# Recurrent level products that stream the queries' columns only

## The chip, the cores and the metric

The kernel runs on one core of one Trainium2 chip. The metric is the device time of one launch in microseconds (us), as the median of several runs. The engines are named as the profile names them: PE is TensorE's matmul, PEld its weight load (the load of the stationary operand into the array), DVE is VectorE, ACT is ScalarE, POOL is GpSimd, SP is SyncE, which issues the transfers.

## The reference, cut to what matters

The program computes two transformer-like blocks, one after the other, on 1024 tokens of width 1024. The change touches one part of the second block, a gated linear recurrence with 4 heads of width 128, run forwards and backwards:

```python
causal = jnp.tril(jnp.ones((HG_CHUNK, HG_CHUNK), bool))[:, :, None]
...
    b = jnp.cumsum(gc, axis=2)
    inter = jnp.einsum('bhtk,bhkv->bhtv', qc * jnp.exp(b), s)
    diff = b[:, :, :, None, :] - b[:, :, None, :, :]
    decay = jnp.where(causal, jnp.exp(jnp.minimum(diff, 0.0)), 0.0)
    scores = jnp.einsum('bhtk,bhtsk,bhsk->bhts', qc, decay, kc)
    intra = jnp.einsum('bhts,bhsv->bhtv', scores, vc)
```

A score between query t and key s holds a decay that differs for each of the 128 features, so the scores aren't one plain matrix product.

## The kernel before

The kernel is a sequence of stages. `stage_hgrn` computes the recurrence in 8 units, `units[n] = (h, d)`: head h (0 to 3), direction d (0 forwards, 1 backwards); even n are forwards. The 1024 tokens lie along the free axis, the 128 features across the partitions, in 8 chunks of 128 tokens.

The scores of a chunk are built from 7 levels, `LEVELS = [64, 32, 16, 8, 4, 2, 1]`, and a diagonal. At a level with runs of m tokens the chunk is cut into blocks of 2m; one half of each block holds keys, the other queries. For d = 0 the keys are the left half and the queries the right, for d = 1 the other way round. Both are decayed to the middle of their block, so that one float32 matmul of the buffer with itself holds all scores between the two halves. Level 0 (m = 64) has one block in a chunk: 64 adjacent key tokens and 64 adjacent query tokens. At level 6 (m = 1) keys and queries alternate.

For each unit and level:

- DVE subtracts (`subtract`, L3198/L3199 or L3202/L3203) and ACT takes the exponential (L3034), in one of three buffers `x`.
- DVE multiplies the keys' half (L3211) and the queries' half (L3212) in (`weigh`). The second of these raises `x_ready`.
- PE waits for `x_ready` in `level`, then issues 8 matmuls, one for each chunk, 128 stationary columns against 128 moving columns (L2914). Each float32 matmul is two weight loads and two passes in the records, so a level is 16 of each.
- DVE copies the scores that the mask of this level names into `att` (`select`, L3229). It reads the queries' columns of PSUM only. The diagonal (L3237) is taken first, from a product of its own (L2935).

PE's jobs rotate over three pairs of PSUM banks (`slot`: job number modulo 3), so a job starts only when the job three before it has been read (`wait_free`). PE's order in unit n is written out by hand: transposes of the decayed keys (L2932), the diagonal's product (L2935), levels 0 and 1, in units 2, 4 and 6 a sum of squares (L2922), the chunks' states (L2945), the projections Z0 and Z1 of unit n+1 (L200), levels 2 and 3, the product with the states (L2956), the projection V0 when unit n+1 begins a head, level 4, the other projections of unit n+1 (GATE for a backwards unit, V1 and QUERY for a forwards one), levels 5 and 6, and then, after `selected`, the product of the scores with the values (L2967). `selected` is raised by DVE when `select` of level 6 is done.

After Z1, ACT and DVE prepare unit n+1: ACT takes out Z1 (L2980), three activations (L3015 to L3017), DVE L3147 to L3149, and, after ACT's L3026 to L3028 (`forget_parts`, which comes behind the take-out of V0 in ACT's order), DVE's `forget` (L3158 to L3166) and `key_distance` (L3176), with `select` of levels 5 and 6 behind that. In some other stages PE runs narrower products: L2668 has 128 stationary columns and one moving column, L475 one or two stationary columns and 64 moving ones in four column groups in turn, L1336 64 stationary columns in two column groups in turn.

Of the kernel before, what the change touches and what calls it, by code (L numbers as in the profile page):

```python
# [26 lines left out]
P = 128  # L27
T = 1024
# [37 lines left out]
LEVELS = [64, 32, 16, 8, 4, 2, 1]  # L66
# [751 lines left out]
class SsmParams:  # L818
# [26 lines left out]
    def product(self, out, a, b, t):  # L845

        link, tt = self.link, self.dve.tensor_tensor
        link(tt(t[0], a[0], b[0], ALU.mult))
        link(tt(t[1], a[1], b[1], ALU.mult))
        link(tt(t[2], a[0], b[1], ALU.mult))  # L850
        link(tt(t[3], a[1], b[0], ALU.mult))
        link(tt(out[0], t[0], t[1], ALU.subtract))
        link(tt(out[1], t[2], t[3], ALU.add))
# [1910 lines left out]
def stage_hgrn(k):  # L2764
# [13 lines left out]
    def take(*shape):  # L2778
        v = k.ar(at[0], *shape)
        at[0] += int(np.prod(shape))  # L2780
        return v
# [4 lines left out]
    keys, b = take(2, TT), take(2, TT)  # L2786
# [11 lines left out]
    units = [(h, d) for h in range(HG_HEADS) for d in range(2)]  # L2798
# [27 lines left out]
    def slot(job):  # L2826
        i = jobs.index(job)
        return i % 3, i // 3

    def banks(job):  # L2830
        s, _ = slot(job)
        return k.ps[:, 2 * s:2 * s + 2, :].rearrange("p b n -> p (b n)")
# [4 lines left out]
    def wait_free(pe, job):  # L2837
        s, use = slot(job)
        if use >= 1:
            pe.wait_ge(read[s], use)  # L2840
# [13 lines left out]
    def buffer(n, l):  # L2854
        return (NL * n + l) % 3
# [7 lines left out]
    out = k.second_out = OutProjection(k, "w_out_2", None, 16 * T, B_FREE, first_raw=k.ar(B_FREE + 2 * T, 2, KD, P),  # L2863
                                       first_tile=HG_HEADS)
# [4 lines left out]
    with nc.Block() as block:  # L2869
# [13 lines left out]
        def _(pe):  # L2883
# [21 lines left out]
            def chunk_job(job, chunks, fn):  # L2905
                wait_free(pe, job)
                for i, c in enumerate(chunks):
                    last = fn(banks(job)[:, i * P:(i + 1) * P], c)
                last.then_inc(made[slot(job)[0]], 1)

            def level(n, l):
                pe.wait_ge(x_ready, NL * n + l + 1)
                v = x[:, buffer(n, l), :]
                chunk_job((n, "level", l), range(T // P), lambda out, c: pe.matmul(  # L2914
                    out, v[:, c * P:(c + 1) * P], v[:, c * P:(c + 1) * P], start=True, stop=True))

            def sum_of_squares(n, h):
                pe.wait_ge(sq_done, h)
# [9 lines left out]
            for n, (h, d) in enumerate(units):  # L2928
                halves = (range(8), range(8, NCH))
                pe.wait_ge(kh_ready, n + 1)  # L2930
                for i in range(2):
# [4 lines left out]
                    out, keys[:, n % 2, CTX + c * P:CTX + (c + 1) * P], q[:, h % 2, c * P:(c + 1) * P],  # L2936
                    start=True, stop=True))
                level(n, 0)
                level(n, 1)
                if d == 0 and h:  # L2940
                    sum_of_squares(n, h)
# [5 lines left out]
                front(n + 1, Z0)  # L2947
                front(n + 1, Z1)
                level(n, 2)
                level(n, 3)  # L2950
                pe.wait_ge(states_ready, n + 1)
# [3 lines left out]
                for c in range(T // P):  # L2955
                    last = pe.matmul(o_ps[:, c * P:(c + 1) * P], states[:, c, :], qh[:, c * P:(c + 1) * P],  # L2956
                                     start=d == 0 and c % 4 == 0, stop=False, skip_group_check=True)
# [8 lines left out]
                for c in range(T // P):  # L2966
                    last = pe.matmul(o_ps[:, c * P:(c + 1) * P], vals[:, h % 2, CCH + c, :], att[:, c * P:(c + 1) * P],  # L2967
                                     start=False, stop=d == 1, skip_group_check=True)
# [728 lines left out]
```

## Time and profile before

| what | value |
|---|---|
| median of the 3 runs | 2686.35 us |
| lowest and highest run | 2682.31 and 2688.17 us |
| span of the profiled execution | 2683.6 us |
| PE busy, share of the span | 2515.2 us, 94% |
| DVE, ACT busy | 1618.7 us, 961.3 us |
| `stage_hgrn`'s units | about 1398 to 1830 us |
| level products, L2914 | 448 matmuls as 896 passes |

For the profiled execution only the span from first to last instruction is given; it lies 2.75 us under the median of the runs and 1.3 us over the fastest of them. Busy times are unions of the recorded intervals. The mean of one instruction holds its latency and overlaps with its neighbours, so the pace of a stream of n equal instructions is read as (busy time of the group minus one duration) / (n - 1).

### The profile page before, as it was taken

To read this page: it belongs to the slowest core of one execution; us is meant where nothing else is said; L and a number is where in the kernel's file an instruction comes from. 1 tells how busy PE (TensorE), PEld (TensorE's weight loads), DVE (VectorE), ACT (ScalarE), POOL (GpSimd) and SP (SyncE) were. 2 spreads that over 40 slices of the span, in tenths; PEclk is the share of its full clock that TensorE was granted. 3 is DMA by queue.
4 is the path that set the end of the run, shared out by engine and by line. 5 is a ranking of instruction groups with operands and counts; after the bars stand their busy time and mean duration, and the time that the engine had idled before them with its cause. 6 is when DMAs were issued, how large, how long until landed. Compare 5 with 4: busy or idle time off the path is not lost. (4 is left out here: it accounts for less than half of the span.)

```text
span 2683.6 us, 39352 instructions
## 1 busy us (share of the span) xinstructions
PE 2515.2 (94%) x16713; PEld 1353.8 (50%) x16713; DVE 1618.7 (60%) x2104; ACT 961.3 (36%) x1116; POOL 26.9 (1%) x60
## 2 busy tenths in 40 slices
PE   7988788999999999999989999988979999999997
PEld 3456564444444444443566776764434444444443
DVE  6687647554444443654447778786766776674253
ACT  5116317432323231423254656563442222222131
POOL 0000000020000000000000000000000000000000
PEclk9999999999999999999999999999989999999999
DMA  9035474111211124432010000002001111123332
GB/s 324 23 99 184 157 228 147 32 32 51 59 47 47 47 80 111 115 94 87 20 32 16 25 24 25 25 16 63 27 15 49 51 47 47 53 62 102 108 102 91
DMA packets 301591, 198.99 MB, mean 74 GB/s; under 512 B 11248, under 2 KB 296078, under 8 KB 301071
## 3 DMA queue, kind: packets, MB, share of 16 engines
q1 hardware_dynamic: 300582, 196.70, 24.8%
q8 instruction: 105, 1.72, 0.3%
q10 hardware_dynamic: 873, 0.32, 0.0%
q14 instruction: 31, 0.25, 0.0%
HBM read 187.02 MB, written 9.45 MB: 73 GB/s over the span
## 5 line engine op out<-in xcount | busy, mean ns | idle before, releaser
L200 PE MATMUL ps<-hT,arena 128*128 128x512 bf16 (+1 forms) x6384 | 1370.9, 377 | 26.4 <-DVE arena L2086 9.9
L200 PEld LDWEIGHTS ps<-hT,arena 128*128 128x128 bf16 x6384 | 624.2, 98 | 770.6 <-issue 32.4
L1907 PE MATMUL ps<-arena 128*128 128x512 bf16 x2112 | 458.7, 379 | 2.7 <-DVE arena L1889 2.5
L1907 PEld LDWEIGHTS ps<-arena 128*128 128x128 bf16 x2112 | 206.3, 98 | 251.8 <-DVE arena L1889 4.9
L2159 DVE SCALAR_TENSOR_TENSOR arena<-ps,vec,arena 128x945 f32<-128x945 f32 (+2 forms) x176 | 215.1, 1222 | 75.0 <-ACT arena L2145 55.6
L2126 DVE SCALAR_TENSOR_TENSOR arena<-ps,vec,arena 128x1023 f32<-128x1023 f32 (+1 forms) x88 | 106.8, 1275 | 179.6 <-ACT arena L2116 179.6
L1889 DVE TENSOR_TENSOR arena<-hT,arena 128x2816 bf16<-128x2816 f32 (+2 forms) x44 | 93.7, 2157 | 164.4 <-ACT arena L1883 164.2
L1883 ACT ACTIVATE arena<-hT 128x2816 bf16<-128x2816 f32 (+2 forms) x44 | 77.8, 1798 | 237.2 <-DMA hT<-w_down_dram 109.5
L2914 PE MATMUL ps<-arena 128*128 128x128 f32 x896 | 109.4, 279 | 12.2 <-DVE arena L3212 11.4
L2073 DVE TENSOR_TENSOR arena<-hT,arena 128x2048 bf16<-128x2048 f32 x44 | 100.9, 2293 | 28.2 <-ACT arena L2040 27.9
L2116 ACT ACTIVATE arena<-ps,vec 128x1024 f32<-128x1024 f32 x44 | 50.6, 1200 | 175.3 <-PE ps L200 175.3
L2914 PEld LDWEIGHTS ps<-arena 128*128 128x128 f32 x896 | 105.3, 194 | 15.5 <-DVE arena L3212 12.9
L2168 ACT ACTIVATE arena<-arena 128x1024 f32<-128x1024 f32 x22 | 23.2, 1056 | 227.2 <-DVEq L2163 227.2
L2086 DVE TENSOR_TENSOR arena<-arena 128x1024 f32 (+1 forms) x44 | 53.9, 1225 | 59.9 <-ACT arena L2052 59.9
L3229 DVE COPY_PREDICATED arena<-masks,ps 128x512 f32<-128x512 uint32 x56 | 49.4, 883 | 62.2 <-PE ps L2914 61.8
L2040 ACT ACTIVATE arena<-hT 128x2048 bf16<-128x2048 f32 x44 | 83.3, 1894 | 8.2 <-DMA hT<-w_up_dram 8.2
L200 PE MATMUL ps<-arena,hT 128*128 128x128 bf16 (+1 forms) x1152 | 78.5, 231 | 6.4 <-PEq L160 6.4
L200 PEld LDWEIGHTS ps<-arena,hT 128*128 128x128 bf16 x1152 | 74.3, 99 | 10.4 <-issue 6.9
L3034 ACT ACTIVATE arena<-arena 128x1024 f32<-128x1024 f32 x56 | 58.3, 1052 | 56.7 <-DVE arena L3203 41.8
L604 ACT ACTIVATE arena<-xT 128x512 f32<-128x512 f32 x64 | 39.8, 630 | 107.8 <-DVE xT L567 54.9
L2980 ACT ACTIVATE arena<-ps 128x1024 f32<-128x1024 f32 (+1 forms) x48 | 36.1, 753 | 118.0 <-PE ps L200 114.6
L1062 PE MATMUL ps<-arena 128*128 128x512 f32 x160 | 71.7, 602 | 0.5
(431 smaller groups left out, 2522.2 us busy)
## 6 DMA issues: line engine op xcount, KB each, us to landing
xT<-ada_w_dram SPq DMA_DIRECT2D x24, 1024.0 KB, 5.5
hT<-w_up_dram SPq DMA_DIRECT2D x44, 512.0 KB, 5.0
hT<-ffn_up_dram SPq DMA_DIRECT2D x44, 512.0 KB, 5.0
hT<-w_down_dram SPq DMA_DIRECT2D x30, 704.0 KB, 7.0
hT<-ffn_down_dram SPq DMA_DIRECT2D x30, 704.0 KB, 6.9
arena<-w_in_dram SPq DMA_DIRECT2D x35, 512.0 KB, 4.1
xT<-w_mod_dram SPq DMA_DIRECT2D x16, 1024.0 KB, 5.8
arena<-w_mod_dram SPq DMA_DIRECT2D x8, 1024.0 KB, 19.4
```

The lines of the kernel that those rows point to most:

```text
L200: last = pe.matmul(out, lhs(a, kt), rhs(b, kt, i), start=start and kt == 0 and (a, b) == (0, 0), stop=stop and kt == n_k - 1 and (a, b) == ...
L1062: last = pe.matmul(k.ps[:, 2 * p + half, :], exact[n][:, kt, :], h[:, kt, half * HALF:(half + 1) * HALF], start=kt == 0, stop=kt == KD - 1)
L1883: last = act.activation(parts[0], raw, ACT.Copy)
L1889: last = dve.tensor_tensor(parts[1], raw, parts[0], ALU.subtract)
L1907: last = pe.matmul(self.bank(u), self.part(u, a, kt), self.g[:, b, kt, cols], start=kt == 0 and (a, b) == (0, 0), stop=kt == FT - 1 and (a ...
L2040: act.activation(self.w[:, b, :, 0], self.raw, ACT.Copy).then_inc(self.hi[b], 1)
L2073: dve.tensor_tensor(self.w[:, b, :, 1], self.raw, self.w[:, b, :, 0], ALU.subtract).then_inc(self.lo[b], 1)
L2086: dve.tensor_tensor(self.g[:, 1, 2 * i + b, :], c[0], self.g[:, 0, 2 * i + b, :], ALU.subtract).then_inc(self.done[b], 1)
L2126: last = eng.scalar_tensor_tensor(c[s][:, lag:T], p[s][:, 0:T - lag], w[:, tap, s, bass.ds(j, 1)], c[s][:, lag:T], ALU.mult, ALU.add)
L2159: eng.scalar_tensor_tensor(to, src[:, r0 + di:r1 + di, c0 + dj:c1 + dj], w[:, 3 * (di + 1) + dj + 1, bass.ds(j, 1)], to, ALU.mult, ALU.add ...
L2914: chunk_job((n, "level", l), range(T // P), lambda out, c: pe.matmul(out, v[:, c * P:(c + 1) * P], v[:, c * P:(c + 1) * P], start=True, st ...
L3034: act.activation(v, v, ACT.Exp).then_inc(exp_done, 1)
```

## The change

Each level product now streams only the queries' columns of a chunk (64 of the 128, every second run of m), and writes them to the columns of PSUM where they stood before, leaving the keys' columns unwritten. The stationary operand stays all 128 columns, except at level 0, where only the 64 columns of the keys are loaded; their scores go to the 64 PSUM partitions (0 to 63 forwards, 64 to 127 backwards) where they stood before. The number and the order of all instructions and waits stay as they were.

```diff
             def level(n, l):
                 pe.wait_ge(x_ready, NL * n + l + 1)
+                d, m = units[n][1], LEVELS[l]
                 v = x[:, buffer(n, l), :]
-                chunk_job((n, "level", l), range(T // P), lambda out, c: pe.matmul(
-                    out, v[:, c * P:(c + 1) * P], v[:, c * P:(c + 1) * P], start=True, stop=True))
+                rows = slice(d * m, (d + 1) * m) if 2 * m == P else slice(0, P)
+                queries = lambda chunk: chunk.rearrange("p (b h r) -> p b h r", h=2, r=m)[:, :, 1 - d, :]
+
+                def product(out, c):
+                    chunk = v[:, c * P:(c + 1) * P]
+                    return pe.matmul(queries(out[rows, :]), chunk[:, rows], queries(chunk), start=True, stop=True)
+
+                chunk_job((n, "level", l), range(T // P), product)
```

## Rows read from the trace of the kernel before

**Rows 1.** The page's costliest groups: busy us, mean ns of one, then idle before
```profile
L2914 PE MATMUL ps<-arena 128*128 128x128 f32 x896 | 109.4, 279 | 12.2 <-DVE arena L3212 11.4
L2914 PEld LDWEIGHTS ps<-arena 128*128 128x128 f32 x896 | 105.3, 194 | 15.5 <-DVE arena L3212 12.9
```

**Rows 2.** Waits from 1400 to 1860 us: us in total, times, longest
```profile
DVE arena L3229 <- PE ps L2914: 61.8, 17, 7.1
...
PE ps L2967 <- DVEq L3320: 21.9, 8, 3.7
...
PE ps L2914 <- DVE arena L3212: 11.4, 8, 5.1
```

**Rows 3.** Timeline around the end of unit 0 and into unit 1: start, duration (us)
```profile
1439.90 3.73 PE L2914 MATMUL ps<-arena 128*128 128x128 f32 x32
...
1443.15 1.49 DVE L3176 TENSOR_TENSOR arena<-arena 128x1280 f32<-128x1280 f32 x1
...
1444.56 2.68 DVE L3229 COPY_PREDICATED arena<-masks,ps 128x512 f32<-128x512 uint32 x2
...
1447.35 3.78 PE L2967 MATMUL ps<-arena 128*128 128x128 f32 x16 [3.71 <-DVEq L3320]
...
1454.66 1.95 PE L2914 MATMUL ps<-arena 128*128 128x128 f32 x16
...
1456.60 0.68 DVE L3212 TENSOR_TENSOR arena<-arena 128x512 f32<-128x512 f32 x1
...
1457.34 2.05 PE L2914 MATMUL ps<-arena 128*128 128x128 f32 x16 [0.73 <-DVE arena L3212]
...
1460.22 0.72 DVE L3229 COPY_PREDICATED arena<-masks,ps 128x512 f32<-128x512 uint32 x1
...
1461.46 13.14 PE L200 MATMUL ps<-hT,arena 128*128 128x512 bf16 x72
```

**Rows 4.** Timeline of the later part of unit 1 and into unit 2
```profile
1490.72 1.02 ACT L2980 ACTIVATE arena<-ps 128x1024 f32<-128x1024 f32 x1 [6.24 <-PE ps L200]
...
1507.38 1.31 DVE L3229 COPY_PREDICATED arena<-masks,ps 128x512 f32<-128x512 uint32 x1 [0.86 <-PE ps L2914]
...
1511.12 2.05 PE L2967 MATMUL ps<-arena 128*128 128x128 f32 x16 [1.98 <-DVEq L3320]
...
1516.02 2.02 PE L2914 MATMUL ps<-arena 128*128 128x128 f32 x16
...
1516.78 1.22 DVE L3237 TENSOR_TENSOR arena<-ps,ident 128x1024 f32<-128x1024 f32 x1
...
1519.25 2.05 PE L2914 MATMUL ps<-arena 128*128 128x128 f32 x16 [1.21 <-DVE arena L3212]
```

**Rows 5.** Timeline at 1322 us, a product with one moving column
```profile
1322.17 0.85 PEld L2668 LDWEIGHTS ps<-ones,arena 1*128 1x128 f32 x7 [0.24 <-issue]
```

**Rows 6.** Timeline at 192 to 194 us, products with few stationary columns
```profile
192.31 0.42 PEld L1336 LDWEIGHTS ps<-arena 128*64 128x64 f32 x8 [0.33 <-issue]
...
193.33 1.07 PE L475 MATMUL ps<-xT,cact 128*1 128x64 f32 x64
```

**Rows 7.** Lines L1336 and L475: instructions, min/median/max ns, first and last start
```profile
L1336 PEld LDWEIGHTS ps<-arena x240: 132/137/230, 192.3 to 276.5; 128*64 128x64 f32 x120
```
```profile
L475 PEld LDWEIGHTS ps<-xT,cact x2560: 79/85/129, 189.6 to 407.8; 128*2 128x2 f32 x118, 128*1 128x1 f32 x79
L475 PE MATMUL ps<-xT,cact x2560: 216/219/314, 189.6 to 407.9; 128*2 128x64 f32 x118, 128*1 128x64 f32 x79
```

**Rows 8.** Busy us of PE, PEld, DVE, ACT, POOL; PEclk, DMA share, GB/s
```profile
207.00:209.00 2.00, 0.19 (x11) 0.10 (x2) 1.83 (x4) 2.00 (x9) 0.00 (x0) 1.00 0.37 96
...
211.00:213.00 2.00, 2.00 (x16) 1.35 (x16) 0.19 (x2) 2.00 (x10) 0.00 (x0) 0.50 0.30 100
```
```profile
1447.00:1449.00 2.00, 1.66 (x8) 1.66 (x8) 1.78 (x3) 0.00 (x0) 0.00 (x0) 0.50 0.01 4
...
1508.00:1511.00 3.00, 1.13 (x11) 0.94 (x9) 3.00 (x4) 1.34 (x2) 0.00 (x0) 1.00 0.56 163
```

## The prediction

> **What bounds the kernel now.** I read the page first: PE is busy in 94% of the span, and the level products, L2914, hold 109.4 us of it, with weight loads for 105.3 us at the same time [rows 1]. That is the most that a change of L2914 could touch. Next come the waits in the recurrent stage. PE waits there in two places only: before L2967 for `selected` (21.9 us in all), and before a level product for DVE's L3212 (11.4 us). DVE waits 61.8 us for L2914, but most of that is level 2, which stands behind the long projections in PE's order [rows 2]. So PE and DVE take turns at setting the end, and each level product has to be placed in the timeline.
>
> In units 0, 2, 4 and 6 (read in unit 0) levels 5 and 6 end at 1443.63, while DVE goes straight from L3176 to the two selects (1444.56 to 1447.24) without a wait for them. PE stands 3.71 us and starts L2967 when they are done [rows 3]. Levels 5 and 6 are off the path there. At the start of the next unit level 0 ends at 1456.61, and level 1 starts only at 1457.34, just after L3212 ends at 1457.28: the 0.73 us after level 0 are DVE's. Then PE runs without a gap: level 1, the states, Z0 and Z1 (to 1474.60), levels 2 and 3 [rows 3].
>
> In units 1, 3 and 5 (read in unit 1) more of PE is on the path. Levels 2 and 3 stand before V0, for which ACT waits 6.24 us before it can go on to the next unit's forget gates; and select of level 5 waits 0.86 us for level 5's product. PE's stop before L2967 is 1.98 us [rows 4]. In the next unit level 1 again waits for L3212, 1.21 us [rows 4].
>
> **The change part by part.** *Nothing is added or moved*: the same instructions, waits and transfers, in the same order. What can change is the pace of a pass, and the latency of the last one.
>
> *The pass before.* 32 passes in 3.73 us at 279 ns each: (3730 - 279) / 31 = 111 ns [rows 1, 3].
>
> *Levels 1 to 6 after.* The streamed columns halve, the loaded columns stay 128. What does a float32 pass cost by its two sides? The load: one stationary column takes 85 ns, 64 take 137, 128 take 194 (the 85 being one or two columns) [rows 1, 7]. That is 85 ns of latency and about 0.83 ns a column, so 128 columns keep the load path for some 107 ns. The stream: 64 passes of 64 moving columns in 1.07 us at 219 ns, (1070 - 219) / 63 = 13.5 ns, in four column groups in turn, so 54 ns in one group [rows 6, 7]. Both sides of today's pass are thus about 107 ns, and the change halves only one. The nearest row to what is left is L2668, 128 loaded columns against a single moving column: seven loads in 0.85 us at about 187 ns (between the 137 for 64 columns and the mean of 194), (850 - 187) / 6 = 110.5 ns [rows 5]. A pass with one moving column is as slow as one with 128; with 64 it can't be far from that. I take 110.5 ns, a gain of 0.5 ns, 0.01 us for a level. The bounds: 54 ns, if the load should somehow not hold it (a gain of 16 x 57 = 0.91 us for a level), and something above 111 if the spread-out columns cost more: DVE's select, which reads the same pattern from PSUM, takes 0.72 us at runs of 32, and 1.31 us at runs of 2 [rows 3, 4], a factor of 1.8. Applied to 54 ns that is 97 ns, still under the load. So I take no loss. The last matmul's latency falls from 279 to some 225 ns (219 for 64 columns [rows 7]), so whoever waits for a level is released about 0.05 us earlier.
>
> A rule speaks against this. The Trainium skill, in SBUF — State Buffer, Door 1: The DMA port swizzle, says that PSUM has lines of 8 bytes and that any non-contiguous pattern there significantly slows down matmuls. No run here shows it for a matmul; it gives no figure, and by the load's 107 ns a slower write would have to be over twice slower before it showed. The sum would move by it only if that is so.
>
> *Level 0 after.* 64 columns loaded (137 - 85 = 52 ns [rows 7]) and 64 streamed (54 ns): 55 to 60 ns a pass, so 16 x 54 = 0.86 us less. Going over to another division of the array costs something: the load before L1336 stood 0.33 us with nothing to wait for [rows 6]. Net about 0.5 us in each unit. All of it goes into the wait behind it: level 1 can't start before L3212, which waits for the diagonal's product and exponentials, not for level 0. The wait of 0.73 us becomes about 1.3, that of 1.21 about 1.7 [rows 3, 4]. The cover is DVE's diagonal and weigh work; were it gone, the term would be worth 8 x 0.5 = 4 us.
>
> *The sum.* On the path lie level 1 in seven units, levels 2, 3 and the release by level 5 in units 1, 3 and 5, and some of the last unit: 3 x (0.05 + 0.05 for V0's earlier start and small pace gains) + 7 x 0.02 + 0.1 = about 0.5 us. The profiled execution's span of 2683.6 us would become 2683.1; against the median of the runs that is 2686.35 - 0.5 = 2685.8 us. What a measurement of this kernel can tell from no change is about 0.2%, 5.4 us.
>
> **The rivals.** *The stream sets the pace (faster).* Then each level is 0.91 us shorter, plus 0.05. For it: 64 streamed columns take 54 ns in L475 [rows 6, 7]. Against it: L2668's 110.5 ns [rows 5]. In the units after an even one only level 1 counts, and Z0 can't begin before select of level 1 has read its banks, 1460.94 against 1461.46 now [rows 3]: about 0.4 us. In units 1, 3 and 5 V0 ends 0.4 + 2 x 0.91 = 2.2 us earlier and the 0.86 us wait for level 5 goes too: 3.1 us. Sum 3 x 3.1 + 4 x 0.4 + 1 for the last unit = 12 us: 2674 us. But PE's stop before L2967 in the odd units then grows from 1.98 to nearly 4 us, and after 3.71 us the even ones run L2967 at half clock (below), about 2 us each: 2680 us. The Trainium skill, in TensorE: Matmul & The Clock Gate, Back-to-back issue gap, gives the isolated gap by the moving columns alone, while its section LDWEIGHTS gives a load by its columns, 128 / 1.2 ns; the first would give this rival, the second the forecast, and the trace's loads agree with the second (107 ns).
>
> *The clock falls more often (slower).* The even units show what it costs: after the stop of 3.71 us the granted clock is 0.50, 1.2 GHz [rows 8], and L2967 takes 3.78 us against 2.05 in unit 1 [rows 3, 4]. From its start to that of level 0 it is 7.31 us (1447.35 to 1454.66) against 4.90 (1511.12 to 1516.02), with the same work between. That is 2.4 us for a fall. In the odd units a stop of 1.98 us leaves the clock at 1.00 [rows 4, 8]. But it is close: at 207 to 209 us PE stood 1.8 us, and the clock was 0.50 at 211 to 213 us although PE had been at work since [rows 8]. After the change PE streams only half of the time in the levels on either side of the stops, and the stops after level 0 grow by 0.5 us. The place is the odd units' stop before L2967; the point from which it decides is a fall there in each of the three: 3 x 2.4 = 7 us, less up to 0.7 us each, since DVE comes to L3237 only at 1516.78 in any case [rows 4]: 5 to 7 us, 2691 to 2693 us. Falls after level 0 in all units, where the states and Z0 would run at half clock, would give up to another 7 x 2 = 14 us, 2707. Against it: the same stops as now, and weight loads busy throughout.
>
> *The spread columns cost more than the load hides (slower).* It decides from 111 ns a pass on; at 160 ns, 0.8 us a level, with levels 4 and 5 on the path in three units, it would be 5 us. I count it with the last.
>
> **How the numbers follow.** Load-bound, clock as now: 0.58, around 2685.8, its own range 2680 to 2690 by the runs' own scatter. Stream-bound: 0.17, 2674 to 2680. Clock or columns: 0.25, 2691 to 2707, most of it near 2693. The range 2677 to 2697 takes in the first, the milder part of the faster one and most of the slower one. Faster by over 0.2% (under 2681): 0.18. Slower (over 2691.7): 0.24. Within: 0.58.
>
> **What the profile after would show.** Right: L2914's loads stay near 100 us busy with 1.8 us for a level; level 0 alone near 1.1 us; the wait for L3212 up by some 4 us; the stop before L2967 unchanged at 3.7 and 2.0 us; selects at the same places of a unit. Stream-bound: a level takes 1.1 us, L2914's idle before it doesn't change by that, and units shorten by 0.4 and 3.1 us. Clock: PEclk 0.5 near L2967 in the odd units or behind level 0, with L2967 above 3 us there. The prediction is wrong if a load isn't the floor that L2668 shows, or if half-streamed passes count for less with the clock.

## The result and the profile after

The changed kernel takes 2703.35 us (median of 4 runs, 2698.32 to 2707.68) against 2685.89 us before (4 runs): 1.0066 of before, 95% interval 1.0051 to 1.0082. It is slower by some 17 us, where 2685.8 and at most 2697 had been forecast. The profiled execution has a span of 2696.6 us, 13.0 more than before; it is the fastest of the four, so it shows a little less than the whole loss.

The level products first. They are L2920 now, the other lines of the stage move down by 7 (L2939 are the transposes, L2942 the diagonal's product, L2952 the chunks' states, L2929 the sum of squares, L2963 the product with the states, L2974 the product with the values). These are the page's costliest groups after, in the columns of [rows 1]:

```profile
L2920 PE MATMUL ps<-arena 128*128 128x64 f32 (+1 forms) x896 | 103.3, 273 | 17.6 <-DVE arena L3219 17.0
...
L2920 PEld LDWEIGHTS ps<-arena 128*128 128x128 f32 (+1 forms) x896 | 100.5, 190 | 20.9 <-DVE arena L3219 19.0
```

Half of the columns are gone, and 6 us of 109 with them. The wait for DVE's last multiplication (L3219, which was L3212) grew by 5.6 us, about as much. (The 103.3 us hold some 2 us of level 1 at half clock, in units 3 and 5.) So PE's own work and wait at this line cancel, as forecast, and the 13 us must be elsewhere.

The timeline after, PE alone, at the start of unit 1, to be laid beside [rows 3]:

```profile
1453.87 1.15 PE L2920 MATMUL ps<-arena 128*64 128x64 f32 x16
1456.51 2.00 PE L2920 MATMUL ps<-arena 128*128 128x64 f32 x16 [1.49 <-DVE arena L3219]
1458.34 4.08 PE L2952 MATMUL ps<-arena 128*128 128x128 f32 x20
...
1475.24 3.68 PE L2920 MATMUL ps<-arena 128*128 128x64 f32 x32
```

Level 0 takes 1.15 us instead of 1.95, and the stop behind it 1.49 instead of 0.73. Levels 2 and 3 take 3.68 us instead of 3.74, at 64 columns a pass. Between them stands the loss: L2952, which the change doesn't touch, takes 4.08 us for its 20 passes. Before, the same product (L2945) took 2.40 us, with the clock at 1.00:

```profile
1459.23 2.40 PE L2945 MATMUL ps<-arena 128*128 128x128 f32 x20
```
```profile
1457.00:1460.00 3.00, 2.66 (x23) 2.66 (x24) 3.00 (x6) 0.87 (x1) 0.00 (x0) 1.00 0.02 5
```

What happened to it after is in the table by stretches (columns as in [rows 8], the granted clock is the number behind POOL's):

```profile
1457.00:1459.00 2.00, 2.00 (x18) 2.00 (x18) 2.00 (x5) 0.70 (x1) 0.00 (x0) 0.87 0.03 8
1459.00:1461.00 2.00, 2.00 (x11) 2.00 (x11) 2.00 (x4) 0.36 (x1) 0.00 (x0) 0.50 0.00 0
1461.00:1463.00 2.00, 1.95 (x12) 1.64 (x12) 0.62 (x3) 1.06 (x1) 0.00 (x0) 0.77 0.00 0
```

PE is busy all the time, and the clock drops to 0.50, 1.2 GHz, while it works. In the 2 us at that clock 11 passes go through, against 18 in the 2 us before, at 0.87. Three other places after:

```profile
1511.81 2.62 PE L2974 MATMUL ps<-arena 128*128 128x128 f32 x16 [1.98 <-DVEq L3327]
...
1574.61 3.68 PE L2920 MATMUL ps<-arena 128*128 128x64 f32 x16 [1.87 <-DVE arena L3219]
1578.08 4.03 PE L2952 MATMUL ps<-arena 128*128 128x128 f32 x20
...
1762.22 3.63 PE L2929 MATMUL ps<-arena,ones 128*128 128x512 f32 x4
```

The first is the stop between two units, 1.98 us as before, but the product behind it takes 2.62 us instead of 2.05 [rows 4], and the transposes behind it (L2939) 2.34 us instead of 1.25. The others stand behind level 1. The seven intervals between the starts of the product with the values sum to 394.5 us (1446.58 to 1841.12), against 379.4 before (1447.35 to 1826.75), 15.1 us more. That is more than the whole difference of the spans; the rest of the kernel is 2 us shorter in this execution. Unit 2 has no fall behind level 1. In units 1, 3, 4, 5, 6 and 7 the stretch from the start of level 1 to the start of level 2 is 1.6, 3.2, 1.7, 1.6, 1.7 and 1.6 us longer than before, 11.5 us together. The last unit loses 1.5 us more in L2963. Behind the slow L2974 of units 1, 3 and 5 the stretch up to the next level 1 is 0.96 us longer each, 2.9 us together; the other differences are under 1 us each and nearly cancel.

### The profile page after: what moved, and what is told of

It is laid out like the page before. It is cut to its first block and busy times, and to the rows that moved or that the text cites. A ratio compares the mean times of both kernels' runs of the same rounds, so it can differ in the third digit from the quotient of the medians.

```text
span 2696.6 us, 39175 instructions
## 1 busy us (share of the span) xinstructions
PE 2509.7 (93%) x16536; PEld 1361.3 (50%) x16713; DVE 1619.1 (60%) x2104; ACT 961.7 (36%) x1116; POOL 26.9 (1%) x60
## 5 line engine op out<-in xcount | busy, mean ns | idle before, releaser
L200 PE MATMUL ps<-hT,arena 128*128 128x512 bf16 (+1 forms) x6255 | 1357.1, 376 | 36.4 <-DVE arena L2086 9.9
L2920 PE MATMUL ps<-arena 128*128 128x64 f32 (+1 forms) x896 | 103.3, 273 | 17.6 <-DVE arena L3219 17.0
L2920 PEld LDWEIGHTS ps<-arena 128*128 128x128 f32 (+1 forms) x896 | 100.5, 190 | 20.9 <-DVE arena L3219 19.0
```

What stands on the lines that cost most here:

```text
L200: last = pe.matmul(out, lhs(a, kt), rhs(b, kt, i), start=start and kt == 0 and (a, b) == (0, 0), stop=stop and kt == n_k - 1 and (a, b) == ...
L2920: return pe.matmul(queries(out[rows, :]), chunk[:, rows], queries(chunk), start=True, stop=True)
```

## The experiments

All ratios are to the kernel before on the same chip, with 95% intervals. Each diff is against the changed kernel, unless the text says that it is against the kernel before. A fall is a place where the clock goes to half and the products take longer; each timeline shows one execution. "Theory 1" is that passes that stream half of the time bring the clock down near PE's stops, "Theory 2" that the longer stop after the coarsest level does.

**Levels 1 to 6 changed, level 0 as before.**

```diff
-                rows = slice(d * m, (d + 1) * m) if 2 * m == P else slice(0, P)
-                queries = lambda chunk: chunk.rearrange("p (b h r) -> p b h r", h=2, r=m)[:, :, 1 - d, :]
+                rows = slice(0, P)
+                queries = lambda chunk: chunk if l == 0 else chunk.rearrange("p (b h r) -> p b h r", h=2, r=m)[:, :, 1 - d, :]
```

> Levels 1 to 6 stream the queries' columns only; level 0 is as in the kernel before. Theory 1 (passes that stream half of the time bring the clock down at the stops near them): PE still stops 2.0 us before L2967's product in the odd units between two half-streamed levels, and the clock falls there as in the changed kernel, and behind level 1 in most units: 1.004 to 1.007 of before. Theory 2 (the longer stop after the coarsest level does it): that stop is back at 0.7 to 1.2 us, so 1.000 to 1.002.

Measured: 1.0013 (1.0004 to 1.0022). Six of seven levels are as in the changed kernel and four fifths of the loss are gone. Nothing falls behind level 1 (L2952 takes 2.39 to 2.45 us in all units); the odd units' product with the values takes 2.9 to 3.8 us, and the last unit's L2963 3.68 us:

```profile
1459.35 2.00 PE L2920 MATMUL ps<-arena 128*128 128x64 f32 x16 [0.82 <-DVE arena L3219]
1461.18 2.45 PE L2952 MATMUL ps<-arena 128*128 128x128 f32 x20
...
1513.02 3.40 PE L2974 MATMUL ps<-arena 128*128 128x128 f32 x16 [1.98 <-DVEq L3327]
```

Taken alone this speaks for Theory 2.

**Level 0 changed alone.**

```diff
-                queries = lambda chunk: chunk.rearrange("p (b h r) -> p b h r", h=2, r=m)[:, :, 1 - d, :]
+                queries = lambda chunk: chunk if l else chunk.rearrange("p (b h r) -> p b h r", h=2, r=m)[:, :, 1 - d, :]
```

> Only level 0 is changed (64 columns loaded, 64 streamed); levels 1 to 6 stream all 128 columns. Theory 1: all passes next to the stops stream fully but those of level 0, so the odd units' product with the values stays near 2.05 us and the time near 1.000 to 1.002 of before. Theory 2: the stop after level 0 is 1.4 us long as in the changed kernel, the states' product behind it takes over 3.5 us in half of the units, 1.003 to 1.006.

Measured: 0.9993 (0.9984 to 1.0002), no difference that can be told. The odd units' product with the values is at 2.05 us, as Theory 1 had it. Theory 2's loss doesn't come in the median. The profiled execution is one of the longer ones (2689.54 us against a median of 2684.64). In it units 1, 2 and 3 have falls behind level 0 all the same, after stops of 1.87, 2.10 and 1.88 us; units 4 and 6 stand as long, 2.11 and 2.12 us, and have none. Unit 2:

```profile
1518.48 1.12 PE L2920 MATMUL ps<-arena 128*64 128x64 f32 x16
1521.70 2.52 PE L2920 MATMUL ps<-arena 128*128 128x128 f32 x16 [2.10 <-DVE arena L3219]
1524.02 3.14 PE L2929 MATMUL ps<-arena,ones 128*128 128x512 f32 x4
```

From level 1 to level 2 these three units take 1.6 to 1.7 us too much, 4.9 us together, which is what this execution lies over its median. So the falls can come with level 0 alone, but the median lies where it would without them.

**All levels stream the queries only, level 0 loads 128 columns too.**

```diff
-                rows = slice(d * m, (d + 1) * m) if 2 * m == P else slice(0, P)
+                rows = slice(0, P)
```

> The changed kernel, but level 0 loads all 128 columns too and streams 64. Its level 0 then takes 1.9 us like the others (load-bound) and the stop behind it is 0.7 to 1.2 us again. Theory 1: half-streamed passes are what counts, so no better than the changed kernel, 1.005 to 1.008 of before. Theory 2: the stop is short again, so 1.000 to 1.002.

Measured: 1.0061 (1.0046 to 1.0076), the whole loss. The timeline at the start of unit 1, and level 1 of unit 4 with the sum of squares behind it:

```profile
1452.60 1.90 PE L2920 MATMUL ps<-arena 128*128 128x64 f32 x16
1455.38 2.00 PE L2920 MATMUL ps<-arena 128*128 128x64 f32 x16 [0.89 <-DVE arena L3219]
1457.22 4.08 PE L2952 MATMUL ps<-arena 128*128 128x128 f32 x20
...
1639.42 2.00 PE L2920 MATMUL ps<-arena 128*128 128x64 f32 x16 [0.78 <-DVE arena L3219]
1641.25 3.39 PE L2929 MATMUL ps<-arena,ones 128*128 128x512 f32 x4
```

Level 0 is as long as before the change, the stop behind it nearly so in unit 1 (0.89 against 0.73 us), and the fall is the same 4.08 us. In units 4 and 6 the stop is 0.78 us, shorter than in the kernel before (1.14 and 1.02 us), which has no fall there, and this run has one. Theory 2 falls with this run: the length of the stop isn't what the change did wrong. Nor is it the narrow load of level 0 or the other division of the array. From the run with levels 1 to 6 (whose stops from unit 1 to unit 6 are 0.73 to 0.97 us; here they are 0.78 to 1.02 us) it differs only in that level 0 streams 64 columns a pass and not 128. Theory 1 is right in that the halved streams count, but as it stood it had expected the loss with levels 1 to 6 alone as well; by the medians, both sides of the stop have to be halved.

**Level 0's products issued twice, all else as changed.**

```diff
+                if l == 0:
+                    wait_free(pe, (n, "level", l))
+                    for c in range(T // P):
+                        product(banks((n, "level", l))[:, c * P:(c + 1) * P], c)
                 chunk_job((n, "level", l), range(T // P), product)
```

> The changed kernel with level 0's products issued twice: 0.9 us more work for PE in each unit, into the stop of 1.44 us behind level 0, nothing later. Without the clock this costs nothing and gains nothing: 1.0066 of before as the changed kernel. If the stop behind level 0 is the cause of the falls behind it (Theory 2), they go and it is faster than the changed kernel by 0.3 to 0.5%, with 0.1 to 0.3% left for the odd units' other falls. By Theory 1 it changes little, 1.004 to 1.007, since level 0's passes stay as sparse as the others.

Measured: 1.0012 (1.0003 to 1.0021). 7 us more work for PE, and by the ratios some 15 us less time than the changed kernel:

```profile
1454.51 2.08 PE L2920 MATMUL ps<-arena 128*64 128x64 f32 x32
1457.09 2.00 PE L2920 MATMUL ps<-arena 128*128 128x64 f32 x16 [0.51 <-DVE arena L3223]
1458.93 2.45 PE L2956 MATMUL ps<-arena 128*128 128x128 f32 x20
```

L2956 (the chunks' states here) is at 2.45 us; the odd units' product with the values still takes 3.4 to 3.8 us. The expectation by Theory 1, 1.004 to 1.007, missed. Its word "sparse" doesn't fit level 0 of the changed kernel: 16 passes in 1.15 us at a mean of 225 ns are (1150 - 225) / 15 = 62 ns a pass of 64 columns, against 111 ns for 128 before. What level 0 has less of is columns, 1024 in all instead of 2048, and this run streams 2048 again. It also shortens the stop, from 1.49 to 0.51 us, so by itself it doesn't tell the columns from the stop; the run before it does.

**Levels 0 and 1 changed, the others as before.**

```diff
+                queries = lambda chunk: chunk if l > 1 else chunk.rearrange("p (b h r) -> p b h r", h=2, r=m)[:, :, 1 - d, :]
```

> Levels 0 and 1 as changed, levels 2 to 6 stream all 128 columns as before. If half-streamed passes bring the clock down where they lie next to a stop, the falls behind level 1 (states' product or sum of squares at 3.3 to 4.1 us) stay, and those at the odd units' product with the values go (2.05 us): 1.003 to 1.006 of before. If all half-streamed passes of a unit add up, nothing falls behind level 1: 1.000 to 1.001.

Measured: 1.0059 (1.0046 to 1.0072). Two of seven levels carry nearly the whole loss. The falls behind level 1 are there in every unit (L2952 at 3.7 to 4.6 us in units 0, 1, 3, 5 and 7, L2929 at 3.3 to 3.7 in units 2, 4 and 6); the profiled execution is the slowest of the five, 2709.72 us against a median of 2701.19. Against the expectation, two of the three odd units' products with the values are still slow (2.82 and 3.23 us) in this execution, though the levels beside that stop stream fully.

**Levels 2 to 6 changed, 0 and 1 as before.**

```diff
-                rows = slice(d * m, (d + 1) * m) if 2 * m == P else slice(0, P)
-                queries = lambda chunk: chunk.rearrange("p (b h r) -> p b h r", h=2, r=m)[:, :, 1 - d, :]
+                rows = slice(0, P)
+                queries = lambda chunk: chunk if l < 2 else chunk.rearrange("p (b h r) -> p b h r", h=2, r=m)[:, :, 1 - d, :]
```

> Levels 0 and 1 as before, levels 2 to 6 as changed. By the first reading the product with the values in the odd units takes 2.6 to 3.8 us, and nothing falls behind level 1: 1.0005 to 1.002 of before, like the kernel with level 0 alone left as before. By the second the falls behind level 1 come back: 1.003 or more.

Measured: 1.0020 (1.0011 to 1.0028), the upper end of the first reading. Nothing falls behind level 1 (L2952 at 2.40 us), the odd units' product with the values takes 2.77 to 3.65 us, and the last unit's products behind the levels are slow. The two halves, 1.0059 and 1.0020, add up to 1.008, a little over the 1.0066 of both together.

**Filling the stop before the product with the values.** Products of ones with ones (L2916 below), into banks that the next job overwrites.

```diff
+                if n < last_unit:
+                    fill(banks((n + 1, "kt", 0)), FILL[n % 2], (n + 1, "kt", 0))
                 pe.wait_ge(selected, n + 1)
...
+            FILL = (14, 7)
+
+            def fill(out, times, job):
+                wait_free(pe, job)
+                for i in range(times):
+                    pe.matmul(out[:, 0:P], k.ones[:, :], k.ones[:, :], start=True, stop=True)
```

> The changed kernel, with 14 (even units) or 7 (odd units) float32 products of ones with ones, 128 columns each, into the free banks of the next job while PE would stop before the product with the values: 3.1 and 1.6 us more work for PE inside stops of 3.8 and 2.0 us. If the clock falls for want of work, it stays at 2.4 GHz there (2.05 us for that product in all units); the falls behind level 1 stay. Faster than the changed kernel by 0.0 to 0.25%: 1.004 to 1.0066 of before. If the falls come from elsewhere, it is no faster, or slower by late starts.

Measured: 1.0084 (1.0071 to 1.0097), above the forecast 1.004 to 1.0066 and no better than the changed kernel (1.0066, 1.0051 to 1.0082), which was not expected. The filling does what it should where it stands (L2983 is the product with the values here, L2927 the levels):

```profile
1447.69 2.05 PE L2983 MATMUL ps<-arena 128*128 128x128 f32 x16 [0.67 <-DVEq L3336]
...
1454.64 1.12 PE L2927 MATMUL ps<-arena 128*64 128x64 f32 x16 [2.02 <-ACT arena L2996]
1457.63 3.68 PE L2927 MATMUL ps<-arena 128*128 128x64 f32 x16 [1.87 <-DVE arena L3228]
```

The product with the values is at 2.05 us in unit 0 too. But PE then comes to level 0 earlier than ACT has read its banks, and waits there 2.02 us. Level 0, with its 1024 columns, lies between two stops of 2 us, and level 1 (3.68 us) runs at half clock from its start. Units 3 to 6 show slow level 1 products in the same way (3.45 to 3.68 us).

**Filling both stops.** 5 such products more between levels 0 and 1.

```diff
                 level(n, 0)
+                fill(banks((n, "level", 1)), 5, (n, "level", 1))
                 level(n, 1)
```

> As the last, and 5 such products more (1.1 us) in the stop of 1.44 us between levels 0 and 1. By the clock theory every fall of the changed kernel inside the stage goes and the whole loss with it: 0.999 to 1.001 of before, though PE does about 30 us more work. If the loss were in the passes or in a wait and not in the clock, it would stay at 1.0066 or grow.

Measured: 0.9993 (0.9984 to 1.0002). 30.9 us of filling in 234 passes, and by the ratios the kernel is some 19 us faster than the changed one (0.73%): no loss can be told any more. The timeline and the clock in the same place as above:

```profile
1452.03 1.12 PE L2927 MATMUL ps<-arena 128*64 128x64 f32 x16 [2.02 <-ACT arena L2997]
1453.07 1.38 PE L2916 MATMUL ps<-ones 128*128 128x128 f32 x10
1455.02 2.00 PE L2927 MATMUL ps<-arena 128*128 128x64 f32 x16 [0.56 <-DVE arena L3229]
1456.85 2.45 PE L2960 MATMUL ps<-arena 128*128 128x128 f32 x20
```
```profile
1453.00:1455.00 2.00, 1.45 (x13) 1.19 (x11) 2.00 (x4) 0.72 (x1) 0.00 (x0) 1.00 0.21 59
1455.00:1457.00 2.00, 1.98 (x17) 1.98 (x18) 2.00 (x4) 0.19 (x1) 0.00 (x0) 1.00 0.00 0
1457.00:1459.00 2.00, 2.00 (x20) 2.00 (x19) 2.00 (x4) 0.86 (x1) 0.00 (x0) 1.00 0.00 0
```

**The kernel before, its stop before the product with the values filled.** The edit is the first filling (14 or 7 products), applied to the kernel before.

> The kernel before with 14 or 7 products of ones before the product with the values. In the kernel before the clock is at half there in the even units. If those falls were on the path, it is faster by up to 4 x 2.4 = 10 us (0.996). By the reading of the traces DVE's work up to the diagonal is as long as PE's cold work, so nothing is won: 0.999 to 1.001. All passes stream 128 columns, so the earlier start of level 0 should bring no fall behind level 1 that costs as much as in the changed kernel with the same filling (1.0084): at most 1.002.

Measured: 0.9997 (0.9988 to 1.0006), as expected. The even units' falls of the kernel before cost nothing: DVE comes to the diagonal no earlier (7.6 us after its last select in unit 0 of both). With 128 columns streamed on both sides the stops at level 0 (2.01 us here, then 0.97) bring no fall. The second stop is shorter than the 1.87 us of the changed kernel so filled.

**Sixteen streamed columns.** The kernel before with a quarter of the changed kernel's columns; the diff is against the kernel before.

```diff
-                    out, v[:, c * P:(c + 1) * P], v[:, c * P:(c + 1) * P], start=True, stop=True))
+                    out[:, 0:16], v[:, c * P:(c + 1) * P], v[:, c * P:c * P + 16], start=True, stop=True))
```

> The kernel before, but each level product streams only the first 16 columns of its chunk, which leaves out seven eighths of every level product (the scores are then incomplete). The load of 128 columns stays. If the load sets the pace, a level of 16 passes stays at 1.8 to 1.9 us (111 ns a pass). If the stream does, it falls to some 0.7 us. If the clock goes by how much is streamed, it falls in more places than in the changed kernel, also behind levels 2 to 4, and the time is 1.008 to 1.02 of before; if it goes by busy weight loads, no worse than 1.002.

Measured: 1.0185 (1.0171 to 1.0199), for an eighth of the streamed work. The page's group and the timeline at the start of unit 3:

```profile
L2914 PE MATMUL ps<-arena 128*128 128x16 f32 x896 | 127.0, 288 | 11.5 <-DVE arena L3212 10.0
```
```profile
1584.19 1.93 PE L2914 MATMUL ps<-arena 128*128 128x16 f32 x16 [0.63 <-ACT arena L2980]
1587.18 3.59 PE L2914 MATMUL ps<-arena 128*128 128x16 f32 x16 [1.06 <-DVE arena L3212]
1590.62 4.00 PE L2945 MATMUL ps<-arena 128*128 128x128 f32 x20
```

At full clock a level still takes 1.93 us with 16 columns: the load of 128 float32 columns sets the pace, whether 128, 64 or 16 are streamed. And with less streamed the clock is at half in more places, also in level 4 (3.43 us) and the product with the states behind level 3 (3.2 to 3.8 us): the levels' busy time rises from 109.4 to 127.0 us.

**All stops filled, the changed kernel and the kernel before.** The edit adds 11 products before level 3 of the last unit and 5 before its last product with the values; the kernel before has 3 instead of 5 between levels 0 and 1.

> The changed kernel with both stops filled (0.9993), and with 11 and 5 such products more in the last unit, before its level 3 and before its last product with the values, where the clock still falls. Those falls cost 3.67, 3.42 and 3.49 us against about 1.95 each; level 3 lies on the path: 0.998 to 0.9995 of before. It would beat both kernels by 0.1% at most; if the last unit's falls are hidden behind DVE, it stays at 0.9993.

> The kernel before with all stops filled in the same way (3 products between levels 0 and 1). If the clock is all that the changed kernel lost, this and the changed kernel so filled come out alike, within 0.1%: 0.998 to 1.0005 of before. If the narrower streams have a value of their own that the clock hid, this one is slower than the changed one so filled by over 0.1%.

Measured: the changed kernel so filled 0.9993 (0.9984 to 1.0002), the kernel before so filled 0.9985 (0.9976 to 0.9994). The last unit's falls of the changed kernel are gone (its level 3 at 2.00 us), yet the time didn't move beyond its interval. The kernel before with the filling is the fastest of all, by 0.15%, just clear of no change; between these two the intervals overlap. No value of the narrower streams shows. The two aren't quite alike in clock: in the profiled execution of the changed kernel so filled, level 0 of units 3, 5 and 7 still runs partly at half clock, 1.73 to 1.92 us instead of 1.12.

## Why the prediction was wrong

**The pace of a pass** was right. The forecast, a float32 pass held at 110.5 ns by its load of 128 columns, was taken from L2668's one-column row. Levels 2 and 3 take 3.68 us after against 3.74, the difference being the last pass's 0.05 us, and with 16 columns a level still takes 1.93 us. The rival in which the stream sets the pace is refuted. The spread-out columns cost nothing either: levels 5 and 6, with runs of 2 and 1, take 3.68 us like levels 2 and 3. The small gains in the sum came too: from the start of level 2 to the product with the values units 1, 3 and 5 are 0.10 to 0.11 us shorter than before.

**Level 0** was right in kind: 1.15 us instead of 1.95, 0.8 us less where 0.5 net was forecast, and all of it went into the wait for L3212 (now L3219), 1.44 or 1.49 us in most units where 1.3 to 1.7 was forecast, and 1.76 and 1.87 in two. The page shows it (the wait grew by 5.6 us), and the level-0-alone run at 0.9993 gains nothing. That PE waits in the stage in two places only was not exact: it also stands 0.8 us for ACT before two level products and 1.1 us before the last sum of squares, and 5.1 us of the 11.4 stand before the last unit's level 3. The sum doesn't hang on it.

**The step that failed** is the sum: it kept the clock as it was ("load-bound, clock as now: 0.58"), with the argument that weight loads would be busy throughout. The loads were back to back and the clock fell all the same: 0.50 from 1459 to 1461 us with PEld busy for 2.00 of 2.00 us. The term for the clock, put at nothing, measured some 17 us. The rival "the clock falls more often" is what happened, at 0.25 with 2691 to 2707 us. Its point of decision was set at the wrong place. It put the sure part at the odd units' stop before the product with the values, 5 to 7 us for three falls. Those falls came, at 0.96 us each, 2.9 us together in the trace. The runs that have them (with the last unit's) and show none behind level 1 come to 1.0012, 1.0013 and 1.0020, 3 to 5 us. The part that it named last and thought the less likely, falls behind level 0 where the states' product runs, at up to 14 us, carries the loss: 11.5 of the 15.1 us in the trace; the run with levels 0 and 1 alone is at 1.0059.

**Why there and not elsewhere.** By the medians two things were needed together, and each was tried alone: half the columns before the stop with full streams behind it (level 0 alone) costs nothing measurable, half the columns behind it with a full level before it (levels 1 to 6) costs 0.13%, none of it behind level 1, both together 0.6%, whether level 0 takes 1.15 or 1.90 us. What follows level 1 is on the path with little slack, states, Z0 and Z1: in unit 1 the fall costs 1.63 us from level 1 to level 2, and the unit is 1.46 us longer from one product with the values to the next (65.23 against 63.77 us). A fall before the diagonal is hidden by DVE in the even units, as filling the kernel before showed (0.9997), and in part in the odd ones.

**What the range left out.** The upper end, 2697, took only the milder part of that rival. The Trainium skill says in TensorE: Matmul & The Clock Gate, in its section "HAM oscillation — how this bites in real kernels", that gaps in PE's work throttle it again. The traces agree that the clock falls behind stops (to 0.50 behind the one of 1.49 us). But a longer stop wasn't needed: with level 0 loading 128 columns, two falls came behind 0.78 us, where the kernel before stands 1.14 and 1.02 us and has none. What had changed there were the columns streamed on both sides.

**Open.** That the loss is the clock's is settled by filling: with it the whole loss goes. How halved streams bring the clock down isn't settled; the runs show only where it falls. Nor is it settled why two odd units' products with the values were slow with levels 2 to 6 streaming fully, or why the profiled execution of the level-0-alone kernel has three falls while its median shows no loss. Each profile is one execution, and falls come and go between executions of one kernel.

## What to carry to other kernels

A float32 product with 128 stationary columns wasn't sped up by streaming fewer than 128 moving columns: with 128, 64 and 16 of them a level took 1.95, 1.90 and 1.93 us, since the load takes as long. Before thinning PE's work in a stretch where it also waits, read the granted clock around the stops and ask what stands behind them; saved columns that end up in a wait can cost the clock of the work behind it. Where a thinned stretch has lost time, refilling the waits with idle products is a quick test of whether the clock is the cause (1.0066 to 0.9993 here), and every such filling has to be placed against what PE waits for next: at one of the two stops alone it gave 1.0084, no gain.

## What the runs showed of the hardware that had not been expected

- Busy weight loads didn't keep the clock up. With fewer columns streamed behind the same loads it fell in more places: 64 columns a pass in all levels gave 1.0061, 16 gave 1.0185, with the loads back to back (busy for 126.8 us of the levels' 127.0).
- A fall can come while PE works without a gap, 0.87 and then 0.50 at 1457 to 1461 us, after a stop of 1.49 us that had ended at 1456.51.
- Adding 31 us of useless products made the changed kernel some 19 us faster (1.0066 to 0.9993), and adding them at the first stop alone gained nothing (1.0084, with an interval that overlaps the changed kernel's).
